# Three attentions of a streaming encoder on TensorE: one merged block in common steps in place of two blocks in sequence

## What is computed

```
z = q k^T / 8                      8 heads of 64
log_keep = -softplus(z) where key < query, else 0
log_between = (sum of log_keep over the later keys)
weight = exp(log_sigmoid(z) + log_between) where key < query, else 0
o = weight v
```

## Time and profile before

| | us |
|---|---|
| time, median of 3 runs (4415.27 to 4425.43) | 4424.21 |
| the profiled execution's own time | 4421.1 |
| its span (first to last instruction) | 4419.2 |
| TensorE busy in the span | 3611.0 |
| VectorE busy | 2811.9 |
| GpSimd busy | 1836.7 |
| ScalarE busy | 1235.3 |

### The profile page before, as it was taken

The page is one execution under the profiler, slowest core; times in us unless marked ns, Lnnn a source line. Parts: engine busy times, 40 slices in busy tenths (PEclk is TensorE's granted clock), DMA queues, the critical chain, the costliest instruction groups (busy, mean ns, idle before and its releaser), DMA issues.

```text
span 4419.2 us, 34952 instructions
## 1 busy us (share of the span) xinstructions
PE 3611.0 (82%) x11113; PEld 1885.0 (43%) x11113; DVE 2811.9 (64%) x6038; ACT 1235.3 (28%) x2663; POOL 1836.7 (42%) x1477
## 2 busy tenths in 40 slices
PE   7999798989768797867898878996787777787777
PEld 4545457778534345432333335442233233233222
DVE  2130541821698965886996997687677676676554
ACT  2111772620332233332223224333111112112111
POOL 0000340000366576656666666666433333333332
PEclk9999996989889999988999999998899999999999
DMA  3202102234799899989999999999999999999998
GB/s 123 69 25 80 30 1 86 84 122 162 293 351 391 319 405 421 396 333 421 421 419 421 412 420 415 422 411 409 421 421 421 417 412 418 415 413 414 421 421 354
DMA packets 249160, 1415.44 MB, mean 320 GB/s; under 512 B 26624, under 2 KB 59648, under 8 KB 95872
## 3 DMA queue, kind: packets, MB, share of 16 engines
q0 software_dynamic: 165888, 1208.03, 66.6%
q1 hardware_dynamic: 83088, 205.18, 12.6%
HBM read 1374.85 MB, written 39.19 MB: 320 GB/s over the span
## 4 chain that ended last, share of the span: by engine, by line
DMA 23%; POOL 18%; DVE 13%; PE 12%; issue 11%; ACT 2%; POOLq 0%; SPq 0%; ACTq 0%; DVEq 0%
DMA ring<-in_experts_dram,idx 22%; POOL side L1265 10%; POOL ring L1254 8%; PE ps L1375 7%; DVE ring L1618 5%; PE ps L1298 2%; PE ps L1323 1%; DVE wgt L1624 1%; PE ps L1346 1%; PE ps L1308 1%; ACT diag L1468 1%; DVE hot L1507 1%; DVE hot L1510 1%; DVE e L1512 1%; DVE flat L1503 0%
## 5 line engine op out<-in xcount | busy, mean ns | idle before, releaser
L1375 PE MATMUL ps<-ring,diag 128*128 128x512 f32 x3520 | 1792.9, 654 | 688.4 <-ACT diag L1468 667.1
L1254 POOL DMA_INDIRECT ring<-in_experts_dram,idx x1152 | 1096.1, 952 | 1905.9 <-PE ps L1375 1334.5
L1618 DVE CUSTOM_DVE_ANT_0 ring<-ring,ps 128x1024 f32<-128x1024 f32 x1152 | 1381.7, 1217 | 556.1 <-DMA ring<-in_experts_dram,idx 548.7
L1375 PEld LDWEIGHTS ps<-ring,diag 128*128 128x128 f32 x3520 | 695.3, 206 | 1693.2 <-ACT diag L1468 948.7
L1265 POOL TENSOR_TENSOR side<-side,ring 128x1024 f32<-128x1024 f32 x272 | 640.8, 2356 | 42.6 <-ACT ring L1473 37.4
L1457 ACT ACTIVATE act_<-hid 128x2 f32<-128x2 f32 x576 | 117.1, 203 | 1773.5 <-DVE hid L1618 1772.8
L1468 ACT ACTIVATE diag<-const,wgt 128x128 f32<-128x128 f32 x880 | 319.4, 395 | 482.8 <-DVE wgt L1624 480.2
L1298 PE MATMUL ps<-hx,wbuf 128*128 128x256 f32 (+2 forms) x1152 | 403.1, 495 | 13.3 <-DMA hx<-hT_scratch 13.1
L1624 DVE TENSOR_TENSOR wgt<-act_,gw 128x2 f32<-128x2 f32 x576 | 240.9, 418 | 124.9 <-ACT act_ L1457 121.6
L1473 ACT ACTIVATE ring<-ring,wgt 128x1024 f32<-128x1024 f32 x272 | 308.4, 1134 | 0.0
L1298 PEld LDWEIGHTS ps<-hx,wbuf 128*128 128x128 f32 x1152 | 225.6, 196 | 184.5 <-issue 119.3
(11 more groups left out here) (187 smaller groups left out, 3096.6 us busy)
## 6 DMA issues: line engine op xcount, KB each, us to landing
wbuf<-in_w_gate_o_dram SPq DMA_DIRECT2D x72, 768.0 KB, 8.3
wbuf<-in_w_q_dram SPq DMA_DIRECT2D x24, 1024.0 KB, 9.0
ring<-in_experts_dram,idx POOLq DMA_INDIRECT x1152, 16.0
wbuf<-in_w_out_dram SPq DMA_DIRECT2D x12, 1024.0 KB, 8.9
w_qkv<-in_w_in_dram SPq DMA_DIRECT2D x5, 2048.0 KB, 8.0
o_x<-o_scratch SPq DMA_DIRECT2D x9, 768.0 KB, 25.2
s<-s_scratch SPq DMA_DIRECT2D x6, 1024.0 KB, 11.6
hT_scratch<-hT SPq DMA_DIRECT2D x9, 512.0 KB, 7.0
```

The source lines that it names most:

```text
L1254: i = nc.gpsimd.indirect_dma_start(out=ring[:, j % RING, :], out_offset=None, in_=A["experts"], in_offset=bass.IndirectOffsetOnAxis(ap=idx ...
L1375: last = nc.tensor.matmul(acc[:, h, :], diag[:, (by_pe(j) - 1) % 4, :], ring[:, j % RING, DM + h * HB:DM + (h + 1) * HB], start=(j % SLOTS ...
L1618: last = nc.vector.tensor_tensor_reduce(out=u, in0=u, in1=xp, scale=1.0, scalar=0.0, op0=ALU.mult, op1=ALU.add, accum_out=hid[:, j % SLOTS ...
```

## The change

`stick` and `windows` become one block, `attend`. A class `Course` lays out 108 common steps (tau); each engine goes through them and does, in a fixed order, what falls on that step.

- Stick works in halves: a half covers the four heads of one parity, 512 columns, one half per step, and one step is left free after each tile. Scores fall on step b, softplus on b + 1, suffix sums and exponential on b + 2, values on b + 5.
- The suffix sums are added by TensorE to the logits in their own PSUM bank (three banks in rotation), and ScalarE takes the exponential from there. The copy of z and VectorE's addition are gone. The sum over later blocks is VectorE's, in halves, and so are the masks; GpSimd has nothing to do in this block.
- A window unit starts every third step (every fourth after a memory unit). It has one score buffer (banks 4 and 5), its transposes go in two parts through bank 6, and its values to bank 7.
- The caches of keys come as inputs that are already laid out transposed; TensorE's transposes and ScalarE's copies of them are gone. Their products with the sample's queries fall on four steps behind the last prompt tile. The cached memory keys and values pass through two buffers of one sequence each.
- hT is stored to its scratch during `project`, ahead of the fifth unit's store on SyncE's list.

Cut to its core:

```diff
+                if t == 4 and c == 0:
+                    sp.wait_ge(h_done, NX)
+                    for i in range(NT):
+                        sp.dma_start(hT_d[i], hT[:, :, i * P:(i + 1) * P]).then_inc(spilled, 16)
...
+class Course:
+    def __init__(self):
+        self.steps = []
+        b = 0
+        for t in range(NT):
+            kbs = list(range(t, -1, -1)) if t < ST else [ST, None]
+            for k, kb in enumerate(kbs):
+                self.steps.append((t, kb, k == 0, k == len(kbs) - 1, b))
+                b += 2
+            b += 1
+        every = [(k, p, x) for k, x in enumerate(self.steps) for p in range(2)]
+        at = lambda lag, ok=lambda x: True: {x[4] + p + lag: (k, p) for k, p, x in every if ok(x)}
+        self.score, self.soft, self.suffix, self.values = at(0), at(1), at(2), at(5)
+        self.plain = at(2, lambda x: not x[2])
+        self.least, self.dexp, self.mask = (at(lag, lambda x: x[2]) for lag in (2, 3, 4))
+        self.late = at(3, lambda x: not x[3])
+        self.okeep = {x[4] + 6: k for k, x in enumerate(self.steps) if x[3]}
+        self.units = [(t, c) for t in range(NT) for c in range(3)]
+        self.win = []
+        b = 1
+        for t, c in self.units:
+            if t == ST and c == 0:
+                self.mul_at = b + 4
+                b = self.mul_at + 6
+            self.win.append(b)
+            b += 4 if c == 2 else 3
+        wat = lambda lag: {b + lag: u for u, b in enumerate(self.win)}
+        self.wscore, self.wfront, self.wexp, self.wnorm = wat(0), wat(1), wat(2), wat(3)
+        self.wturn = {b + 4 + k: (u, k) for u, b in enumerate(self.win) for k in range(2)}
+        self.wvalues, self.wkeep = wat(6), wat(7)
+        self.mul = {self.mul_at + k: k for k in range(4)}
+        u, b = len(self.win) - 1, self.win[-1]
+        del self.wvalues[b + 6], self.wkeep[b + 7]
+        self.past_values = {b + 6 + k: k for k in range(4)}
+        self.wkeep[b + 10] = u
+        self.length = max(max(self.okeep), max(self.wkeep)) + 1
...
+        za = sb("za", [P, 2, HB])
+        wts = sb("wts", [P, 4, HB])
+        sps = sb("sps", [P, 3, HB])
+        later = sb("later", [P, 2, HB])
+        cache = sb("cache", [P, 4 * DM])
...
+        PTs = sb("PTs", [P, 4 * 2 * P])
+        kwcT = sb("kwcT", [P, DB, P])
+        vwc = sb("vwc", [P, DB, P])
+        kmem = sb("kmem", [P, 2, DM])
+        mx = sb("mx", [P, 3, 8, 4])
...
+            sp.dma_start(bias[:, :, :].rearrange("p h k -> p (h k)"), wide_dram[:, 0:BW]).then_inc(bias_in, 16)
+            sp.dma_start(sink[:, :], A["sinks"][0:1, :].to_broadcast([P, SWH])).then_inc(sink_in, 16)
+            sp.dma_start(kcache, A["cache_kT"]).then_inc(kc_in, 16)
+            sp.dma_start(kwcT[:, :, :].rearrange("p b s -> p (b s)"), A["cache_swa_kT"]).then_inc(kw_in, 16)
+            sp.dma_start(vwc[:, :, :], A["cache_swa_v"][0].rearrange("b s h d -> s b (h d)")).then_inc(kw_in, 16)
+            for b in range(2):
+                sp.dma_start(kmem[:, b], A["cache_mem_kT"][b]).then_inc(km_in[b], 16)
...
+                if tau in C.mul:
+                    k = C.mul[tau]
+                    for b in range(2 * k + 2, 2 * k + 4):
+                        sp.wait_ge(mul_done, b - 1)
+                        if b < DB:
+                            sp.dma_start(kmem[:, b % 2], A["cache_mem_kT"][b]).then_inc(km_in[b % 2], 16)
+                        else:
+                            load_vm(b - DB)
+                if tau in C.past_values:
+                    k = C.past_values[tau]
+                    if k < 3:
+                        for b in range(2 * k + 2, 2 * k + 4):
+                            sp.wait_ge(pv_part, b - 1)
+                            load_vm(b)
...
+            for tau in range(C.length):
+                if tau in C.suffix:
+                    k, p = C.suffix[tau]
+                    x = C.half(k, p)
+                    pe.wait_ge(sp_ready, x + 1)
+                    z = ps[:, x % 3, :]
+                    last = nc.tensor.matmul(z, tri, sps[:, x % 3], start=False, stop=True, skip_group_check=True)
+                    if not C.steps[k][2]:
+                        pe.wait_ge(latered, C.lates(k - 1, p) + 1)
+                        last = nc.tensor.matmul(z, negones, later[:, p], start=False, stop=True, skip_group_check=True)
+                    last.then_inc(sums, 1)
+                if tau in C.wscore:
+                    u = C.wscore[tau]
+                    t, c = C.units[u]
+                    if u >= 1:
+                        pe.wait_ge(w_exped, u)
...
+                if tau in C.values:
+                    k, p = C.values[tau]
+                    t, kb, first, end, _ = C.steps[k]
+                    x = C.half(k, p)
+                    if first:
+                        pe.wait_ge(masked, C.sort(k, p) + 1)
+                        if p == 0 and t:
+                            pe.wait_ge(st_kept, t)
+                    else:
+                        pe.wait_ge(weighed, C.sort(k, p) + 1)
+                    if kb is None:
+                        pe.wait_ge(vc_in, 16)
+                    w = wts[:, x % 4]
+                    for j in range(4):
+                        h = 2 * j + p
+                        out = ps[p * HD:(p + 1) * HD, 3, j * P:(j + 1) * P]
+                        if kb is not None:
+                            last = nc.tensor.matmul(out, v[:, kb, h * HD:(h + 1) * HD], w[:, j * P:(j + 1) * P],
+                                                    start=first and j == 0, stop=end, skip_group_check=True)
+                            continue
...
+                if tau in C.wturn:
+                    u, half = C.wturn[tau]
+                    if half == 0:
+                        pe.wait_ge(normed, u + 1)
+                    if u or half:
+                        pe.wait_ge(pt_kept, 2 * u + half)
+                    for k in range(4 * half, 4 * half + 4):
+                        last = nc.tensor.transpose(ps[:, 6, (k % 4) * P:(k % 4 + 1) * P], L[:, u % 3, k // 2, (k % 2) * P:(k % 2 + 1) * P], ident)
+                    last.then_inc(w_turned, 1)
+                if tau in C.wvalues:
+                    u = C.wvalues[tau]
+                    t, c = C.units[u]
+                    pe.wait_ge(pt_kept, 2 * u + 2)
+                    if u:
+                        pe.wait_ge(w_kept, u)
...
+                if tau in C.past_values:
+                    m = C.past_values[tau]
+                    if m == 0:
+                        pe.wait_ge(pt_kept, 2 * NU)
+                        pe.wait_ge(w_kept, NU - 1)
+                    for b in range(2 * m, 2 * m + 2):
+                        pe.wait_ge(km_in[b % 2], 16 * (DB // 2 + b // 2 + 1))
...
+                if tau in C.score:
+                    k, p = C.score[tau]
+                    t, kb, _, _, _ = C.steps[k]
+                    x = C.half(k, p)
+                    r = slice(p * HD, (p + 1) * HD)
+                    z = ps[:, x % 3, :]
+                    if x >= 3:
+                        k3, p3 = (x - 3) // 2, (x - 3) % 2
+                        pe.wait_ge(minned if C.steps[k3][2] else weighed, C.sort(k3, p3) + 1)
+                    if kb is None and p == 0:
+                        pe.wait_ge(kc_in, 16)
+                    for j in range(4):
+                        if kb is not None:
+                            last = nc.tensor.matmul(z[:, j * P:(j + 1) * P], kT[r, j, kb * P:(kb + 1) * P], qT[r, j, t * P:(t + 1) * P],
+                                                    start=(j == 0), stop=True, skip_group_check=True)
+                            continue
...
+                if tau in C.plain:
+                    k, p = C.plain[tau]
+                    x = C.half(k, p)
+                    act.wait_ge(sums, x + 1)
+                    if x >= 4:
+                        act.wait_ge(pv, x - 3)
+                    nc.scalar.activation(wts[:, x % 4], ps[:, x % 3, :], ACT.Exp).then_inc(weighed, 1)
...
+                    a = za[:, x % 2]
+                    nc.scalar.activation(a, ps[:, x % 3, :], ACT.Abs).then_inc(absd, 1)
+                    act.wait_ge(absd, x + 1)
+                    nc.scalar.activation(a, a, ACT.Exp, scale=-1.0).then_inc(zexped, 1)
+                    act.wait_ge(zexped, x + 1)
+                    nc.scalar.activation(a, a, ACT.Ln, bias=1.0).then_inc(logd, 1)
...
+                if tau in C.late:
+                    k, p = C.late[tau]
+                    x = C.half(k, p)
+                    dve.wait_ge(sums, x + 1)
+                    if C.steps[k][2]:
+                        nc.vector.tensor_copy(later[:, p], sps[:, x % 3]).then_inc(latered, 1)
+                    else:
+                        dve.wait_ge(latered, C.lates(k - 1, p) + 1)
+                        nc.vector.tensor_tensor(later[:, p], later[:, p], sps[:, x % 3], ALU.add).then_inc(latered, 1)
+                if tau in C.least:
+                    k, p = C.least[tau]
```

(92 more changed lines are left out.)

661 lines of the change are left out of this document (244 added, 417 removed).

## The result

The changed kernel takes 4463.36 us (median of 4 runs, 4461.75 to 4472.59), the kernel before, beside it on the same chip, 4419.74 (4411.49 to 4425.43). The ratio is 1.0104, with a 95% interval of 1.0081 to 1.0128: slower by 44 us. The forecast was 4459, or 35 us more than before.

The account below looks back on a forecast made before the run. Both stages, once settled, were taken as TensorE back to back. 395 + 20 + 38 + 34 + 26 + 31 + 4.3 = 549 us for 513.5, +35, gave 4459 us; range to hold 8 in 10: 4415 to 4502.

Parts of the forecast that it names:

- One-sided groups: Prompt's stick halves: scores and values on one array half lose their overlap, 0.43 + 0.43 us more per half, 62 us.
- Switches: Prompt's stick halves: three switches between matmul shapes at about 0.20 us each, 36 more times 0.62, 22 us.
- The prompt part: Merged block to the last prompt tile: 395 us of TensorE work, plus 20 of stalls at diagonals and start.
- The sample's part: After the last prompt tile: stick part 38, key stage 34, three units 26, past values 31, end 4.3 us.
- the tile's stick part: Sample tile's stick work: same records as before, 41.6 us before, 38 now.
- The key products: Sample's key stage: transposes and first-load wait go, 4.2 us for each of eight sequences, 34 for 60.1.
- The three units: Sample's window units, alone with one score buffer where there were two: 26 us for 19.4 before.
- Past values: Sample's past values: two buffers refilled meanwhile, 8.4 us per pair, 31 us; 23.6 if loads were hidden.
- hT's store: Store moved into the projection: zero cost, 10 us at most if exposed.
- (a): Rival, stick halves still overlap on the array: the 62 us don't arise, 4397 us; chance 0.11.
- (b): Rival, covers break: VectorE's window fronts delay suffixes and ScalarE's exponentials the logits, add 45, 4504 us; chance 0.17.
- (c): Rival, the sample's small matmuls run at full clock: 33 us less, no change, 4426 us; chance 0.10.

Follow-up runs that it names:

- both whole: Changed kernel with the scores of a step's two halves issued together, and their values too: 4411.99 us, ratio 0.9973 to the kernel before.
- the last experiment: Kernel before with transposed key caches and hT's nine stores moved into the projection: 4393.83 us, ratio 0.9953 to the kernel before.

## Why the prediction was right, and where its terms were off

The mechanism was right: the attentions were bound by TensorE before, the split into halves makes its matmuls dearer, and what the merge hides is less than that. In size the block came out 43 us longer where 35 was put. Point by point:

- **One-sided groups, +62.** Right. The half was put at 4.05 us and measured 4.02. Undoing both groups takes 66 us off TensorE's busy time in the prompt part, for the 76 of this term and two thirds of the next. In the block's time it is 52.9 us, because whole groups bring waits back.
- **Switches, +22.** The price of 0.20 us each is borne out by the 4.02 us. What they cost in all was not separated; grouping by shape takes out some of them and 9 us of TensorE's busy time, at 0.15 us where it can be read.
- **The prompt part, 395 of work and 20 of stalls.** Measured 394.5 busy and 12.0 idle, 9 us less than forecast. The 20 were 9 for the diagonals and 8 to 11 for the start. In order of time the idle of the start is 1.69, 2.11 and 1.64 us, 5.4 in sum, and that of the diagonals, from 473 us on, nine waits of at most 0.96 and 6.5 in sum. No wait in it names the bias table's load. That the 395 of work came out to the microsecond is chance: it was priced at full clock throughout, and after the waits of 1.69 and 2.11 us the granted clock is down to 0.51 from 434.6 to 455.0 us. Groups there take about twice as long, by their rows some 8 us more in sum (the stretch stands below the list). Against it, three settled steps with a unit were put at 17.05 us and take 16.70 and 16.90 (700.28 to 716.98 to 733.88), some 5 us less in 24 units, and 4.6 us of the prompt's last values (847.98 to 852.53) lie in the next term's stretch.
- **The sample's part, 133, measured 150.** This is the term that failed in size, by 17, of which 4.6 are those last values of the prompt. What it had wrong first is that it took the tile's stick part over unchanged (38), though this part is cut into halves too: the price of one-sided groups, charged 72 times to the prompt, was left out here. Its scores took 9.6 + 11.9 = 21.5 us in two halves for the 17.6 of the earlier trace rows, and 17.4 again in "both whole". Its past values took 2 x 7.0 us, and 11.0 in "both whole"; the same 128 records took 8.6 in the experiment with the transposed caches, where the clock was still high at their start (0.86 from 698.7 to 703.0), so the halves are 3 of this and the low level, 0.50 from 879.0 to 919.9, the rest. The key products alone came out as put: 2 x 2.2 + 6 x 4.2 + the 3.8 of a late transfer = 33 for 34. The three units took 32.7 for 26. From score to score 9.8 us pass twice, for the 7.6 put: I priced the scores at full clock (2.7), but they follow a stage at half clock and take 4.6; the wait behind them, 5.2 for 4.9, was as put. From the third score to the past values 13.1 us pass (939.52 to 952.64) for 8.4, because the values and turns of the first two units stand there too, which the sum left out; the 2.2 for the copies was hidden behind the stick values. Past values 28.7 for 31, which is luck again: the sum had transfers as the limit at 8.4 us per pair, but TensorE waited only 0.3 to 0.9 us for them and itself took 7.0 per pair, at a granted clock of 0.52, for the 5.9 put. The end 5.2 for 4.3.
- **hT's store, 0.** Right, by the last experiment.
- **Rivals.** (a), overlap between one-sided halves, is wrong as put: eight records took 0.96 and 0.85 us. The 0.3 us at a passage between halves exists, but the changed order with a suffix or other work between its halves has no such passage. (b), broken covers, does not occur in the changed kernel (9.7 us) and does in part as soon as TensorE is faster. (c), full clock in the sample's part, holds for two of eight sequences, the ones right behind the suffix sums, and for no more after the wait of 3.8 us.

```profile
434.60:455.00 20.40, 16.63 (x43) 10.14 (x44) 12.41 (x21) 7.46 (x19) 0.00 (x0) 0.51 0.54 207
```

Too high by 9 and too low by 17 half cancel, and the kernel before measured 4419.74 beside the changed one, 4 us less than the 4424.21 that the forecast stands on: part of the nearness of 4459 to 4463 is luck.

The experiments also split the whole. The two blocks took 514.3 us to the loads of hx; with transposed caches alone they take 487.6 (-27); with the merge and the rest of the change as well, but whole groups, 503.7 (+16); in halves 556.6 (+53). The merge itself is no gain even with whole groups: its prompt part takes 362.5 us where the two stages in sequence, already on transposed caches, take these 235.9 and 114.6:

```profile
430.60:666.50 235.90, 203.86 (x1376) 113.94 (x1376) 113.64 (x95) 179.50 (x184) 93.50 (x44) 0.93 0.13 39
...
752.10:866.70 114.60, 110.46 (x704) 93.39 (x705) 100.46 (x179) 70.57 (x225) 0.00 (x0) 0.94 0.18 53
```

Between them and the merged one lie 12 us. How they divide among more switches, VectorE's part of the masks and sums that GpSimd did (93.5 us), and the order of waits was not tried: the step from the one kernel to the other changes all of these at once.

## What to carry to other kernels

Before cutting a group of matmuls that fill half of the array each, look at which halves stand next to each other: here an order that alternates gave two for the time of one, and a cut by parity gave that up whatever else it hid. Charge that price to every part that is cut, also to the small one that looks unchanged. Merging two stages pays only for idle time of the engine that bounds both, so count that first, and count the work of the other engines again for the case that the merge succeeds. A change of several parts is best priced part by part: here the least conspicuous one, caches that come laid out transposed (laying them out lies outside the launch and its time), was worth 0.6% alone and was buried under the rest.

## What the runs showed of the hardware that was not expected

- Sixteen half-array records of 128 columns last 1.09 us alternating, 1.64 in parity order, and eight of one half 1.09, each with the switch to the next group. The first and the last I had; the 1.64, some 0.3 less than two halves on their own, I can't explain.
- The granted clock falls below full in a stretch of 16-column matmuls though TensorE is back to back and transposes nothing in it: 0.68 from 836.4 to 852.5 us and 0.57 from 852.5 to 867.9, both busy to the last tenth. The same sixteen products take 1.85 us right behind 512-column suffix sums and 3.59 after a wait of 3.8 us, and stay there for the remaining six sequences (0.50 from 879.0 to 919.9, the 1.2 GHz level).
